# The last attention head gets an instruction order of its own: two pairs of score banks, page scores first, output products inside the head

## The reference

```
def diff_attend(q, k, v, q_pos, k_pos, lam):
    s = jnp.einsum('bqhcd,bkhcd->bchqk', q, k).astype(jnp.float32) * A_QK_DIM ** -0.5
    s = jnp.where(q_pos[:, None] >= k_pos[None, :], s, -jnp.inf)
    p = jax.nn.softmax(s, axis=-1)
    a = p[:, 0] - lam * p[:, 1]
    return jnp.einsum('bhqk,bkhv->bqhv', a, v.astype(jnp.float32))

def att_output(a, lam_init, out_g, w_out):
    B, T = a.shape[:2]
    o = rms_norm(a, out_g) * (1.0 - lam_init)
    return o.reshape(B, T, A_V_W).astype(w_out.dtype) @ w_out
```

## Time and profile before

| | |
|---|---|
| median of 3 runs | 1497.05 us (1494.32 to 1499.91) |
| the profiled execution | 1497.92 us, of which 1496.3 us from the first to the last instruction (the span) |
| PE busy, share of the span | 1405.5 us, 94% |
| PEld | 1338.8 us, 89% |
| DVE | 843.7 us, 56% |
| ACT | 524.4 us, 35% |
| POOL | 100.4 us, 7% |
| DMA | 167.86 MB, 112 GB/s on the mean |

### The profile page before, as it was taken

One profiled execution on the slowest core, in us unless ns is written; L12 is line 12 of the kernel. 1 busy time (PEld: TensorE's weight loads), 2 busy tenths in 40 slices (PEclk: granted clock), 3 DMA queues, 4 the chain that ended last, 5 costly groups with the idle time before them and its releaser, 6 DMA issues.

```text
span 1496.3 us, 29742 instructions
## 1 busy us (share of the span) xinstructions
PE 1405.5 (94%) x11874; PEld 1338.8 (89%) x11874; DVE 843.7 (56%) x1277; ACT 524.4 (35%) x856; POOL 100.4 (7%) x138
## 2 busy tenths in 40 slices
PE   5999999788999999999999799997799999999997
PEld 5889899678999999999999688784799999999997
DVE  5465357555566666632245688887446666664221
ACT  4333435234332323232224455555233323232110
POOL 0020012101100000000000110100010000000000
PEclk9999999679999999999999999997899999999999
DMA  5452344212222222322224687773122222233320
GB/s 202 71 150 60 119 115 121 41 58 73 84 86 98 84 97 86 120 100 82 81 78 155 178 271 241 241 256 118 47 85 89 95 93 89 89 103 121 99 89 21
DMA packets 45820, 167.86 MB, mean 112 GB/s; under 512 B 5882, under 2 KB 7210, under 8 KB 45498
## 3 DMA queue, kind: packets, MB, share of 16 engines
q1 hardware_dynamic: 38506, 143.77, 29.5%
q0 software_dynamic: 7248, 23.15, 6.2%
HBM read 155.42 MB, written 11.48 MB: 112 GB/s over the span
## 4 chain that ended last, share of the span: by engine, by line
PE 87%; DVE 4%; issue 3%; ACT 3%; DMA 1%; POOL 0%; DVEq 0%; ACTq 0%; POOLq 0%
PE ps L516 56%; PE ps L567 14%; PE ps L696 2%; PE ps L925 2%; PE ps L943 1%; PE ps L1032 1%; ACT w_hi L1101 1%; PE ps L879 1%; PE ps L1008 1%; PE ps L631 1%; PE ps L928 1%; PE ps L738 1%; PE ps L937 1%; DMA qb<-q_rows 1%; DVE w_lo L1557 1%
## 5 line engine op out<-in xcount | busy, mean ns | idle before, releaser
L516 PE MATMUL ps<-h_hi,w_hi 128*128 128x260 f32 x1616 | 460.2, 285 | 4.9 <-DVE h_lo L1566 4.4
L1557 DVE TENSOR_TENSOR w_lo<-raw,w_hi 128x1024 fp32r<-128x1024 f32 (+1 forms) x189 | 245.3, 1298 | 386.1 <-ACT w_hi L1101 385.8
L516 PE MATMUL ps<-h_hi,w_lo 128*128 128x260 f32 x1616 | 458.5, 284 | 0.0
L516 PE MATMUL ps<-h_lo,w_hi 128*128 128x260 f32 x1616 | 457.1, 283 | 0.0
L516 PEld LDWEIGHTS ps<-h_hi,w_hi 128*128 128x128 f32 x1616 | 306.2, 189 | 6.1 <-issue 4.1
L516 PEld LDWEIGHTS ps<-h_lo,w_hi 128*128 128x128 f32 x1616 | 306.1, 189 | 0.2
L516 PEld LDWEIGHTS ps<-h_hi,w_lo 128*128 128x128 f32 x1616 | 306.1, 189 | 0.0
L1101 ACT CAST w_hi<-raw 128x1024 fp32r<-128x1024 f32 (+1 forms) x189 | 208.2, 1102 | 226.6 <-PE ps L516 218.0
L516 PE MATMUL ps<-a_lo,w_hi 128*128 128x260 f32 x704 | 199.0, 283 | 0.0
L516 PE MATMUL ps<-a_hi,w_hi 128*128 128x260 f32 x704 | 198.7, 282 | 0.0
L516 PE MATMUL ps<-a_hi,w_lo 128*128 128x260 f32 x704 | 198.7, 282 | 0.0
(11 more groups left out here) (381 smaller groups left out, 2104.4 us busy)
## 6 DMA issues: line engine op xcount, KB each, us to landing
raw<-in_w_ffn SPq DMA_DIRECT2D x88, 512.0 KB, 3.5
raw<-in_w_down SPq DMA_DIRECT2D x32, 704.0 KB, 4.1
k_pages<-in_cache_k SPq DMA_DIRECT2D x32, 512.0 KB, 5.0
v_pages<-in_cache_v SPq DMA_DIRECT2D x32, 512.0 KB, 7.0
raw<-in_w_rec_in SPq DMA_DIRECT2D x29, 512.0 KB, 4.5
raw<-in_w_att_kv SPq DMA_DIRECT2D x24, 512.0 KB, 5.1
raw<-in_w_rec_out SPq DMA_DIRECT2D x8, 512.0 KB, 4.4
raw<-in_w_att_q SPq DMA_DIRECT2D x8, 512.0 KB, 3.5
```

Source lines behind the costliest of these rows:

```text
L516: ins = TE.matmul(half(bank, h), w_part[:, buf, w], m_part[:, k_at + k, h * HALF:(h + 1) * HALF], start=start, stop=stop)
L1557: V.tensor_tensor(w_lo[:, n % 2, 0:nk * P], raw[:, n % RAW, 0:nk * P], w_hi[:, n % 2, 0:nk * P].bitcast(F32), ALU.subtract).then_inc(lo_sp ...
```

## The change

The functions `head` on all engines lose their `last` branches and serve heads 0 to 6 alone; their steps are moved into small helpers (`score_rows`, `row_least`, `row_weights`, ...) whose instructions are the same. Behind the loop each engine gets a program for head 7, written out:

- the score products of blocks 0 and 2 go to banks 2 and 3, those of blocks 1 and 3 to banks 0 and 1, and none of them waits for the block before it, only for the block two before;
- VectorE does all four pages before blocks 1 to 3 are combined, and the steps of the page chain follow;
- ScalarE casts the first seven heads into `n_hi` early; VectorE makes the low halves in three separate places;
- the terms of the first half of slabs 0 and 1 are made inside the head: first the two that need no `n_lo`, for heads 0 to 6, then those with `n_lo`, then head 7's;
- `s_new` is made by GpSimd behind `mul3`.

The core of the diff, TensorE first (`out_terms` makes the parts named by its last argument: 0 high by high, 1 `w_lo` by `n_hi`, 2 `w_hi` by `n_lo`):

```diff
+            def out_terms(s, g, ks, terms):
+
+                for k in ks:
                     w = slice(k * P, (k + 1) * P)
+                    for t in terms:
+                        w_part, m_part = ((w_hi, n_hi), (w_lo, n_hi), (w_hi, n_lo))[t]
+                        ins = TE.matmul(half(2 * s, g), w_part[:, (f_out + s) % 2, w],
+                                        m_part[:, k, g * HALF:(g + 1) * HALF],
+                                        start=k == 0 and t == 0, stop=k == KT - 1 and t == 2)
                 return ins
...
+            wait(pe, zA, "se")
+            page_values(H, zP)
+            wait(pe, zD, "a3")
+            wait(pe, zA, "att2")
+            turned_rows(3, zP)
+            wait(pe, zD, "ls")
+            TE.matmul(ps[:, 3, 0:16], ONES, s_sum[:, :], start=True, stop=True).then_inc(zP.sem, 1)
+            value_sums(1, 2, zP)
+            wait(pe, tG, "new1")
+            TE.matmul(ps[:, 1, 0:P], ONES, s_new[:, :], start=True, stop=True).then_inc(tP.sem, 1)
+            wait(pe, eA, "hi1")
+            pe.wait_ge(lo_split, f_out + 2)
+            out_terms(0, 0, range(KT - 1), (0, 1))
+            wait(pe, zA, "att3")
+            value_sums(1, 3, zP)
+            out_terms(1, 0, range(4), (0, 1))
+            wait(pe, zA, "sqo")
+            TE.matmul(ps[:, 4, :], ONES, sq3[:, 2, 0:T], start=True, stop=True).then_inc(zP.sem, 1)
+            out_terms(1, 0, range(4, KT - 1), (0, 1))
+            pe.wait_ge(past_in, 8 * 16)
+            wait(pe, zA, "orow")
+            TE.transpose(ps[:, 6, 0:P], o_rows[:, :], IDENT).then_inc(tP.sem, 1)
+            wait(pe, eD, "lo1")
+            for s in range(2):
+                out_terms(s, 0, range(KT - 1), (2,))
+            wait(pe, tA, "sq")
+            TE.matmul(ps[:, 7, 2 * P:2 * P + 64], ONES, s_r2[:, 0, :], start=True, stop=True).then_inc(tP.sem, 1)
             wait(pe, eD, "lo2")
-            wait(pe, tD, "newc")
-            pe.wait_ge(lo_split, f_out + 2)
             for s in range(2):
-                out_half(s, 0)
...
+                out_terms(s, 0, range(KT - 1, KT), (0, 1, 2))
             wait(pe, tD, "lo")
             for s in range(2):
-                out_half(s, 1).then_inc(slab_done, 1)
+                out_terms(s, 1, range(KT), (0, 1, 2)).then_inc(slab_done, 1)
...
+            wait(act, zD, "x0")
+            row_exps(0, 2, zA)
+            S.copy(n_hi[:, 0:4, 0:T], zq[:, 0:4, 0:T]).then_inc(eA.sem, 1)
+            wait(act, zD, "x1")
+            row_exps(1, 0, zA)
+            wait(act, aD, "mix", H - 1)
+            S.copy(n_hi[:, 4:7, 0:T], zq[:, 4:7, 0:T]).then_inc(eA.sem, 1)
...
+            last_stats(0)
+            last_page(0)
+            last_stats(1)
+            last_page(1)
+            last_combine(0)
+            last_page(2)
+            last_page(3)
+            last_stats(2)
+            last_combine(1)
...
+            wait(pool, zD, "mul3")
+            G.memset(s_new[:, :], 0.0).then_inc(tG.sem, 1)
...
+            for c in range(2):
+                g = slice(64 * c, 64 * c + 64)
+                G.tensor_tensor(s_new[g, :].rearrange("p (b h c) -> p b h c", b=B, c=2)[:, :, :, c],
+                                qs[g, :, :].rearrange("p h b -> p b h"), ks[g, :, :].rearrange("p h b -> p b h"),
+                                ALU.mult).then_inc(tG.sem, 1)
```

More of the change, by code:

```diff
@@ L967, in head @@
                     wait(pe, aA, "orow", h - 1)
-                if not last:
-                    wait(pe, sA_, "sqq", r)
-                    sums(6, 0, sP_)
-                    wait(pe, sA_, "kr", r)
+                wait(pe, aA, "sqq", h)
+                sums(6, 0, aP)
+                wait(pe, aA, "kr", h)
                 part(1, 0, 1)
@@ L1512, in head @@
-                wait(act, sP_, "pv", r)
-                if not (last or isinstance(h, int)) or h:
+                split("att_kv", i, 2 * (h0 + 2), KT)
+                wait(act, aP, "ssq", h)
+                rsqrt(two(rs3[:, 0, :]), pair(6), A_QK, aA, "lrq", h).then_inc(aA.sem, 1)
+                act.wait_ge(slab_done, n0 + 2)
+                act.wait_ge(vn_out, 16 * (h + 1))
+                wait(act, aG, "vs", h)
+                S.copy(two(vn[:, :]), pair(0)).then_inc(aA.sem, 1)
+                copy_t(3)
@@ new lines, in head @@
+                split("att_kv", i, 2 * (h0 + 2) + 1, KT)
+                wait(act, aP, "v3", h)
+                S.activation(sq3[:, 2, 0:T], ps[:, 5, :], ACT.Square).then_inc(aA.sem, 1)
+                wait(act, aD, "sub", h)
+                page_exps(aA)
+                wait(act, aP, "ssk", h)
+                rsqrt(two(rs3[:, 1, :]), pair(2), A_QK, aA, "lrk", h).then_inc(aA.sem, 1)
+                wait(act, aP, "sso", h)
+                rsqrt(rs3[:, 2, 0:T], ps[:, 4, :], P, aA, "lro", h).then_inc(aA.sem, 1)
@@ new lines, in head @@
+                page_least(aD)
+                wait(dve, aD, "smax", h)
+                spread_least(aD)
+                wait(dve, aA, "rq", h)
+                V.scalar_tensor_tensor(out=qn[:, 1 - u, :], in0=at_(zq, h + 1), scalar=g_qn[:, :], in1=rs3[:, 0, :],
+                                       op0=ALU.mult, op1=ALU.mult).then_inc(aD.sem, 1)
+                wait(dve, aP, "mb", h)
+                page_shift(aD)
+                split("att_kv", i, 2 * (h0 + 2), KT)
+                wait(dve, aA, "se", h)
@@ L2167, in _ @@
+                mixed(h, aD)
+                wait(dve, aP, "sum", h)
+                V.tensor_copy(at_(l_all, h, slice(0, 16)), ps[:, 4, 0:16]).then_inc(aD.sem, 1)
             head(0, 0, 0, 0)
```

423 lines of the change are left out of this document (233 added, 190 removed).

## The result

The changed kernel took 1481.6 us (median of four runs, 1479.51 to 1486.19) beside 1496.67 for the kernel before: a ratio of 0.9894, 95% interval 0.9874 to 0.9913. On the 1497.05 of the runs shown ahead that is 1481.2. The forecast was 1486.0 with a range from 1481.5, so the direction and most of the size were right and the range missed the ratio by 0.3 us at its lower end.

The account below looks back on a forecast made before the run. The last head's engine-to-engine chain was taken to bound the kernel; hiding low halves (4.57) and first-half output products (7.42), plus earlier page steps, less new waits, moved 1072.49 to 1061.0, 11.5 us less: 1486.0 us, range 1481.5 to 1490.5.

Parts of the forecast that it names:

- block 3 ends: Last attention block on VectorE in the last head: ends at 1038.4 against 1038.60 before, nothing won here.
- page products end: Page value products on TensorE after block 2 is turned: 1.91 us at full clock, at most twice that, ending at 1039.5.
- output products begin: Block 3 turned, page sums, block 2's values and new-token product on TensorE come first, so output products start at 1042.9.
- fourteen products done: 14 slab 0 output products without low halves: 1.65 us at full clock, twice that at half, done at 1044.55.
- scaling done: End of sum product 1.14, logarithm 0.70, exponential 0.64, scaling 0.75 and hand-offs 0.1 in the last head: 1049.9.
- second half takes: 48 output products behind the sample tail: 5.66 us at full clock to 8.38 as before; end taken as 1061.0.
- round trip of the pages: Pages' output through memory ahead of the transpose: 4.3 to 6.1 us, ending by 1046.1, hidden with 2 us to spare.
- the clock holds through the tail: Rival: full clock through the sample tail, second half 5.66 us, end 1059.5, kernel 1484.9 us; chance 0.20.
- the six products: Head 7's last first-half products, in the middle of the sample tail: said to shorten TensorE's idle pieces.
- slow queue: Rival: TensorE's single order suffers from half clock or a GpSimd lock, 3 to 5.5 us, 1489.4 to 1492; chance 0.14.
- Given back: Rival: the next stage's weights come no earlier and the gain is lost, about 1495 us; chance 0.03.
- slower: Rival: the new-token product waits for GpSimd and holds TensorE's queue, slower only beyond 12 + 11.5 = 24 us; chance 0.03.

Follow-up runs that it names:

- x6: Changed kernel with one pair of score banks for all four blocks, block 3's score products behind block 1's turning: stage 43.99 us, ratio to before 0.9931.
- x4: Changed kernel plus 26 unread products of 128 columns where TensorE idles in the last head: stage 40.78 us, ratio to before 0.9916.
- x7: Changed kernel with s_new's zeroing and two multiplies on VectorE in place of GpSimd: stage 41.38 us, ratio to before 0.9899.
- x2: Changed kernel with head 7's six first-half products behind the sample tail, not in it: stage 41.50 us (repeat 41.60), ratio to before 0.9923.
- x5: Changed kernel with the low halves of the first seven heads behind the scaling again: stage 46.52 us, ratio to before 0.9944.

## Why the prediction was right, and where it was wrong

Times again behind head 7's first score product: forecast (its times less 1018.57, where before had that product), measured in the changed kernel's first trace, and the mean of its three traces.

| step of the prediction | forecast | first trace | mean of three |
|---|---|---|---|
| block 3 ends | 19.83 | 19.77 | 19.77 |
| page products end | 20.93 | 22.66 | 22.66 |
| output products begin, behind the new-token product | 24.33 | 24.15 | 24.53 |
| fourteen products done | 25.98 | 25.92 | 26.30 |
| scaling done | 31.33 | 30.97 | 31.35 |
| sample tail done, second half begins | 35.23 | 34.80 | 35.18 |
| second half takes | 7.2 | 5.84 | 5.84 |
| slab 2 begins | 42.43 | 40.64 | 41.01 |

- **Block 3 and VectorE without idle time: right**, within 0.1 us; x6 shows that it is the second pair of banks that does it.
- **Page products: the choice was wrong and did not cost.** I took 1.91 over its double; they took 3.60. The steps behind them I had partly costed at half clock (values of block 2 1.65, measured 0.91, turning 0.85 against 0.69), and I had added up their whole durations where they overlap: from the end of the page products to the first output product I had 3.39, and it took 1.49. So the error of 1.7 was gone at the new-token product. Two errors cancelled, which is luck; x4 shows that the clock was worth 1.4 us there.
- **Fourteen products, values, scaling, round trip of the pages, GpSimd: right**, to 0.4 us in sum in the first trace and 0.05 on the mean. The transpose did not wait, and from it to the second half there are 5.44 us, under the 6 forecast.
- **The second half: this is the step that failed.** "I take 1061.0, between the two and nearer to the row": 7.2 us, as if the clock would still fall in the tail. In all three traces of the changed kernel, in x6, in x7 and in both of x2 it held, and the 48 products took 5.82 to 5.84 (with the six more of x2, 6.56). That is 1.36 of the 1.42 us by which slab 2 began earlier than forecast on the mean of three traces, so in the stage it is the whole miss; the rival "the clock holds through the tail", with a chance of 0.20, was the true case in this term. The reason that I gave for it there, the six products, fell with x2; why the clock held stays open. The row of 8.38 was also a little too long: it runs to the end of the last product, and to the first product of slab 2 there were 8.22.
- **The range.** 15.9 us off 1497.05 were measured and 11.05 forecast. Of the 4.8 between them, 1.3 is the stage (12.8 against 11.5), and 0.45 a slip in the last sum: 1486.4 less the 0.9 by which the profiled execution lay above the median is 1485.5, not 1486.0. The other 3.1 are not in the stage's traces. They go with the spread ahead of it: the next comparison of the same kernel, 0.9933, came to 1487.0, inside the range. The range had too little for that spread: its lower end stands 1.5 below the 1483.0 of all savings together, where the three runs shown reach 2.7 below their own median. At its other end, 1490.5, it stops short of the 1492 of its own slow queue. With the clock held the forecast would have been that rival's 1484.9, still 3.7 above what was measured.
- **Given back, or slower: neither.** Behind the stage the time is 423.8 to 424.4 in every trace.

By the experiments the parts are worth: first-half products inside the head 4.8, low halves there 5.5, second pair of score banks up to 3.0, pages first 1.35, GpSimd 0. They add up to 14.6, more than the 12.8: each was taken out alone, from one trace, and the first two and the pages cost clock as well when they go.

What stays open: why the clock holds through idle times of 1.40 and 0.79 us in the changed kernel and falls behind the same two in x4, where it had come up some 3 us earlier in the stage (0.91 on the mean of 3.69 us from 19.06: up at about 19.7, against 22.7). I have no run that tells the reason. Each program repeated in two or three traces whether the clock held, while the moment at which the clock came up moved by 0.3 to 1.6 us; that the outcome hangs on where in the stage such a moment falls is a rival that no run here tests.

## What to carry to other kernels

A last stage without work of a next one to fill it should take its own following work inside: products that need only finished operands, split off from those that need late ones. Where a row of products follows a stretch with short idle times, cost it at both clocks and give the two nearly equal chances, since no single row of before decides between them. Measure a change of ten us or less by the stage in the trace, between two marks that both kernels have; a median of four runs carried several us from a part that was never touched.

## What was unexpected of the hardware

- The same 32 page products took 1.91 us at full and 3.60 at half clock, nearly in the ratio of the clocks.
- In three executions of one program the clock came up at 22.7, 23.5 and 24.3 us of the stage, behind the same row of page products, and the stage's length followed it.
- The clock held through idle times of 1.40 and 1.65 us (x2, twice), where before it fell behind 1.87: the 0.82 of the sample tail in the earlier trace rows is 1.5 of 4.23 us at half, so it fell at about 1062.7, when the next idle time of 1.65 had just begun (timeline of TensorE before, whose first product behind that takes 0.58, where the changed kernel's takes 0.39):

```profile
1062.19 0.43 PE L1046 MATMUL ps<-s_r,cst 128*128 128x64 f32 x2 [1.87 <-ACT s_r L1528]
1064.27 0.58 PE L1032 MATMUL ps<-n_hi,w_hi 128*128 128x260 f32 x1 [1.65 <-DVE n_lo L2211]
```

- It fell behind 1.40 and 0.79 in x4 (twice, once half a us into the second half), and in the 5.25 of x5. The length of the idle time alone does not order these.
- Work that nobody reads paid: 16 products of 128 columns in the tail, which had idle time there anyway, brought the second half from 7.39 to 5.86 us.
